# mLSTM output with tokens on the partitions: weighted scores stationary, a one-column denominator per block, and four transposes back

## The reference

```
b      = cumsum(log_sigmoid(f))                 per token i
g_j    = i_j - b_j,   r_i = max(0, max_{j<=i} g_j),   m_i = b_i + r_i
s_ij   = (q_i . k_j) / 8 * exp(g_j - r_i)        for j <= i, else 0
num_i  = sum_j s_ij v_j                          128 values per token
den_i  = sum_j s_ij
h_i    = num_i / max(|den_i|, exp(-m_i))
out_i  = h_i * sigmoid(o_i)
```

## Time and profile before

| | |
|---|---|
| median of 3 executions | 2916.95 us (2909.89 to 2918.77) |
| the profiled execution's own time | 2915.71 us |
| its span from first to last instruction | 2913.9 us |
| PE busy / PEld busy | 2749.6 us (94%) / 2169.3 us (74%) |
| DVE / ACT / POOL busy | 1304.5 us (45%) / 1024.4 us (35%) / 1069.6 us (37%) |
| mean granted TensorE clock | 0.979 of full speed |
| the four heads, layer 1 / layer 2 | 757.79 to 845.34 us / 2200.2 to 2289.2 us of the span |

### The profile page before, as it was taken

One profiled execution on the slowest core, in us unless ns is written; L12 is line 12 of the kernel. 1 busy time (PEld: TensorE's weight loads), 2 busy tenths in 40 slices (PEclk: granted clock), 3 DMA queues, 4 the chain that ended last, 5 costly groups with the idle time before them and its releaser, 6 DMA issues.

```text
span 2913.9 us, 36798 instructions
## 1 busy us (share of the span) xinstructions
PE 2749.6 (94%) x13092; PEld 2169.3 (74%) x13092; DVE 1304.5 (45%) x1596; ACT 1024.4 (35%) x1498; POOL 1069.6 (37%) x450
## 2 busy tenths in 40 slices
PE   6999999999988999999999999999998889999998
PEld 5888877766666787888878888767665667878887
DVE  6333353444655455332353333444454563653322
ACT  3222233555535433222232222244554454332221
POOL 3444444411222343444434444443112223444443
PEclk9999999999989999999999999999998999999999
DMA  3222222211111132223222222232011112222231
GB/s 134 89 99 103 99 87 97 100 45 34 53 45 44 66 108 92 88 100 114 89 73 101 96 100 92 87 108 87 30 44 44 55 44 76 101 92 99 88 119 68
DMA packets 36070, 239.54 MB, mean 82 GB/s; under 512 B 3952, under 2 KB 5232, under 8 KB 13936
## 3 DMA queue, kind: packets, MB, share of 16 engines
q1 hardware_dynamic: 32720, 232.80, 22.7%
q10 hardware_dynamic: 3232, 5.17, 0.5%
HBM read 234.81 MB, written 2.10 MB: 81 GB/s over the span
## 4 chain that ended last, share of the span: by engine, by line
issue 63%; POOL 24%; PE 11%; POOLq 1%; DVE 0%; DVEq 0%
POOL wlo L265 24%; PE bank L1191 4%; PE bank L1192 4%; PE bank L1193 4%; POOLq L264 1%; POOLq L260 1%; DVE hlo L689 0%; DVE x L759 0%; POOL selr L252 0%; DVE hhi L687 0%; POOLq L265 0%; POOLq L256 0%; POOL ones L249 0%; POOL onesm L250 0%; DVEq L759 0%
## 5 line engine op out<-in xcount | busy, mean ns | idle before, releaser
L265 POOL TENSOR_TENSOR wlo<-raw,whi 128x1024 fp32r<-128x1024 f32 (+2 forms) x440 | 1068.0, 2429 | 1825.2 <-ACT whi L298 926.1
L1191 PE MATMUL bank<-hhi,whi 128*128 128x512 f32 x1984 | 798.4, 402 | 48.3 <-POOL wlo L265 36.7
L1193 PE MATMUL bank<-hhi,wlo 128*128 128x512 f32 x1984 | 777.8, 392 | 0.0
L1192 PE MATMUL bank<-hlo,whi 128*128 128x512 f32 x1984 | 777.5, 392 | 0.0
L289 ACT ACTIVATE whi<-raw 128x1024 fp32r<-128x1024 f32 (+1 forms) x232 | 264.0, 1138 | 717.8 <-PE bank L1193 717.6
L1191 PEld LDWEIGHTS bank<-hhi,whi 128*128 128x128 f32 x1984 | 376.4, 190 | 137.9 <-issue 47.2
L1193 PEld LDWEIGHTS bank<-hhi,wlo 128*128 128x128 f32 x1984 | 375.5, 189 | 79.5
L1192 PEld LDWEIGHTS bank<-hlo,whi 128*128 128x128 f32 x1984 | 376.3, 190 | 75.0 <-issue 3.1
L746 DVE TENSOR_TENSOR tmp<-tmp,bank 128x512 f32<-128x512 f32 x80 | 55.0, 688 | 534.0 <-PE bank L1193 534.0
L1191 PE MATMUL bank<-uhi,whi 128*128 128x512 f32 x704 | 274.3, 390 | 0.0
L1193 PE MATMUL bank<-uhi,wlo 128*128 128x512 f32 x704 | 273.9, 389 | 0.0
(11 more groups left out here) (266 smaller groups left out, 3148.9 us busy)
## 6 DMA issues: line engine op xcount, KB each, us to landing
raw<-gu SPq DMA_DIRECT2D x88, 1024.0 KB, 4.8
raw<-dn SPq DMA_DIRECT2D x32, 1408.0 KB, 6.0
raw<-cb SPq DMA_DIRECT2D x48, 768.0 KB, 4.3
raw<-pM SPq DMA_DIRECT2D x16, 1024.0 KB, 4.7
raw<-cq SPq DMA_DIRECT2D x16, 1024.0 KB, 4.8
raw<-pA SPq DMA_DIRECT2D x12, 1024.0 KB, 4.7
raw<-wo SPq DMA_DIRECT2D x8, 1024.0 KB, 4.8
x<-xT ACTq DMA_DIRECT2D x4, 512.0 KB, 9.7
```

The source lines that it names most:

```text
L265: pool.tensor_tensor(wlo[:, s, 0:w], raw[:, j, lo:lo + w], whi[:, s, 0:w].bitcast(f32), ALU.subtract).then_inc(sem["lo_done"], 1)
L1191: mm(outp, wh, mhi, start=start and k == 0, stop=False)
L1192: mm(outp, wh, mlo, start=False, stop=False)
L1193: i = mm(outp, wl, mhi, start=False, stop=stop and k == len(parts) - 1)
```

## The change

1. **Numerator.** The weighted scores become the stationary tile (128x128 blocks of `dm`), the values move: ten matmuls of 128 columns instead of four of 512, 384, 256 and 128. Bank 5 then has the tokens on the partitions.
2. **Denominator.** Blocks of `tmp[:, 4]` are stationary, and two columns of ones move: four small matmuls instead of one of 512 columns. There is one denominator per partition and block.
3. **exp(-m)** is computed once for all heads on 128x16 (tokens on partitions), from four more small transposes, into `st4[:, 0]`; the spreading matmul of m (L1490) and the 128x512 Exp of each head (L548) go. `rows` holds r alone.
4. **DVE** does the two maxima and the reciprocal on 128x4; the product with bank 5 spreads the four reciprocals.
5. **Transposes.** PE transposes the result back into bank 6 (4 of 128x128), and DVE multiplies from there with the gate.
6. **Waits.** PE no longer waits for `h_out` before bank 5; it waits for `h_out` ahead of the transposes, for `h_gated` ahead of the scores in bank 6, and, before the first head, for the one Exp (`em_exp`), which reads bank 4.

```diff
+        row1 = within("row1", VS + 1, [NH, S])
+        em = st4[:, 0].rearrange("p (a h) -> p a h", h=NH)
+        den = st4[:, 1:4, 0:NB]
 ACT
                 act.wait_ge(sem["rt_ready"], me.next("rt_ready"))
+                A(st4[:, 0], bank[4][:, NB * NH:2 * NB * NH], ACT.Exp, scale=-1.0).then_inc(sem["em_exp"], 1)
                 for h in range(NH):
...
-                    act.wait_ge(sem["mm_mm"], me.next("mm_mm"))
-                    if h:
-                        act.wait_ge(sem["h_out"], me.at("h_out", h))
-                    A(tmp[:, 5], bank[6][:], ACT.Exp, scale=-1.0).then_inc(sem["em_exp"], 1)
 DVE
-                dve.tensor_copy(rows[0:NH], tmp[0:NH, 2:4]).then_inc(sem["dve_step"], 1)
+                dve.tensor_copy(rows[0:NH], tmp[0:NH, 2]).then_inc(sem["dve_step"], 1)
...
-                    dve.scalar_tensor_tensor(tmp[:, 5], bank[6][:], -1.0, tmp[:, 5], ALU.mult, ALU.max).then_inc(sem["dve_step"], 1)
+                    sums = bank[6][:, 0:2 * NB].rearrange("p (a b) -> p a b", b=2)[:, :, 0]
+                    dve.scalar_tensor_tensor(den[:, 0], sums, -1.0, em[:, :, h], ALU.mult, ALU.max).then_inc(sem["dve_step"], 1)
-                    dve.tensor_tensor(tmp[:, 5], bank[6][:], tmp[:, 5], ALU.max).then_inc(sem["dve_step"], 1)
+                    dve.tensor_tensor(den[:, 1], sums, den[:, 0], ALU.max).then_inc(sem["dve_step"], 1)
-                    dve.reciprocal(tmp[:, 4], tmp[:, 5]).then_inc(sem["dve_step"], 1)
+                    dve.reciprocal(den[:, 2], den[:, 1]).then_inc(sem["dve_step"], 1)
-                    dve.tensor_tensor(tmp[:, 3], bank[5][:], tmp[:, 4], ALU.mult).then_inc(sem["h_out"], 1)
-                    dve.wait_ge(sem["h_out"], me.next("h_out"))
+                    dve.tensor_tensor(tmp[:, 3].rearrange("p (a b) -> p a b", a=NB), bank[5][:].rearrange("p (a b) -> p a b", a=NB),
+                                      den[:, 2].unsqueeze(2).broadcast_to([P, NB, P]), ALU.mult).then_inc(sem["h_out"], 1)
+                    fill_combine(0, 11 + 4 * h)
                     dve.wait_ge(sem["og_ready"], me.at("og_ready", h + 1))
-                    dve.tensor_tensor(zm[:, 8 + h], tmp[:, 3], zm[:, 8 + h], ALU.mult).then_inc(sem["h_gated"], 1)
+                    dve.wait_ge(sem["h_t"], me.next("h_t"))
+                    dve.tensor_tensor(zm[:, 8 + h], bank[6][:], zm[:, 8 + h], ALU.mult).then_inc(sem["h_gated"], 1)
                     dve.wait_ge(sem["h_gated"], me.next("h_gated"))
-                    fill_combine(0, 11 + 4 * h)
 PE
+                pe.wait_ge(sem["em_exp"], me.at("em_exp", 1))
                 pe.wait_ge(sem["cv_silu"], me.at("cv_silu", 4))
                 for h in range(NH):
...
-                    if h:
-                        pe.wait_ge(sem["h_out"], me.at("h_out", h))
...
-                    mm(bank[6][:], sel(h), rows[:, 1], start=True, stop=True).then_inc(sem["mm_mm"], 1)
                     fill("cb0", 8 + 4 * h)
                     fill("cb0", 9 + 4 * h)
                     pe.wait_ge(sem["d_exp"], me.next("d_exp"))
-                    pe.wait_ge(sem["em_exp"], me.next("em_exp"))
+                    if h:
+                        pe.wait_ge(sem["h_gated"], me.at("h_gated", h))
...
-                    for jt in range(NB):
-                        i = mm(bank[5][:, jt * P:S], zm[:, 4 + h, jt * P:(jt + 1) * P], dm[jt], start=jt == 0, stop=jt == NB - 1)
+                    for it in range(NB):
+                        for jt in range(it + 1):
+                            i = mm(bank[5][:, it * P:(it + 1) * P], dm[jt][:, (it - jt) * P:(it - jt + 1) * P],
+                                   zm[:, 4 + h, jt * P:(jt + 1) * P], start=jt == 0, stop=jt == it)
...
-                    mm(bank[6][:], ones[:], tmp[:, 4], start=True, stop=True).then_inc(sem["den_mm"], 1)
+                    for it in range(NB):
+                        i = mm(bank[6][:, 2 * it:2 * it + 2], tmp[:, 4, it * P:(it + 1) * P], ones[:, 0:2], start=True, stop=True)
+                    i.then_inc(sem["den_mm"], 1)
                     fill("cb0", 11 + 4 * h)
+                    pe.wait_ge(sem["h_out"], me.at("h_out", h + 1))
+                    transposes(bank[6], tmp[:, 3]).then_inc(sem["h_t"], 1)
```

More of the change, by code:

```diff
@@ L150, in build @@
         dm = [tail[0][:, 0:S], tail[1][:, 0:3 * P], tail[1][:, 3 * P:5 * P], tail[0][:, S:S + P]]
-        rows = within("rows", VS, [HD, 2, S], f32r)
+        rows = within("rows", VS, [HD, S], f32r)
+        row1 = within("row1", VS + 1, [NH, S])
+        em = st4[:, 0].rearrange("p (a h) -> p a h", h=NH)
+        den = st4[:, 1:4, 0:NB]
         row0 = within("row0", last, [NH, S])
@@ L195, in build @@
             "cv": 16, "cv_silu": 4, "og_ready": 4, "vm_mm": 8, "vm_ready": 8,
-            "mb_mm": 4, "md_mm": 4, "mm_mm": 4, "d_exp": 4, "em_exp": 4, "sm_mm": 12, "sd_mul": 16, "num_mm": 4, "den_sum": 4, "den_mm": 4,
-            "h_out": 4, "h_gated": 4,
+            "mb_mm": 4, "md_mm": 4, "d_exp": 4, "em_exp": 1, "sm_mm": 12, "sd_mul": 16, "num_mm": 4, "den_sum": 4, "den_mm": 4,
+            "h_out": 4, "h_t": 4, "h_gated": 4,
             "al_mm": 2, "al_abs": 2, "al_e": 2, "al_l": 2, "al_out": 2, "al_b": 2, "sr_ready": 4, "ad_zero": 1,
@@ L988, in _ @@
                 dve.wait_ge(sem["dve_step"], me.next("dve_step"))
-                dve.tensor_tensor(tmp[0:NH, 3], tmp[0:NH, 5], tmp[0:NH, 2], ALU.add).then_inc(sem["dve_step"], 1)
+                dve.tensor_tensor(row1[:], tmp[0:NH, 5], tmp[0:NH, 2], ALU.add).then_inc(sem["dve_step"], 1)
                 dve.memset(rows[:].bitcast(f32), 0.0).then_inc(sem["dve_step"], 1)
@@ L996, in _ @@
                 dve.wait_ge(sem["sel_set"], me.at("sel_set", 1))
-                dve.tensor_copy(rows[0:NH], tmp[0:NH, 2:4]).then_inc(sem["dve_step"], 1)
+                dve.tensor_copy(rows[0:NH], tmp[0:NH, 2]).then_inc(sem["dve_step"], 1)
                 dve.wait_ge(sem["dve_step"], me.next("dve_step"))
-                dve.tensor_tensor(rows[32:32 + NH], tmp[0:NH, 2:4], rows[0:NH].bitcast(f32), ALU.subtract).then_inc(sem["row_m"], 1)
+                dve.tensor_tensor(rows[32:32 + NH], tmp[0:NH, 2], rows[0:NH].bitcast(f32), ALU.subtract).then_inc(sem["row_m"], 1)
                 dve.wait_ge(sem["row_m"], me.next("row_m"))
@@ L1472, in _ @@
                 pe.sem_inc(sem["held"], 1)
-                for a in range(NB):
-                    i = pe.transpose(bank[4][:, a * NH:(a + 1) * NH], row0[0:NH, a * P:(a + 1) * P], ident[0:NH, 0:NH])
+                for e, row in enumerate((row0, row1)):
+                    for a in range(NB):
+                        i = pe.transpose(bank[4][:, (NB * e + a) * NH:(NB * e + a + 1) * NH], row[0:NH, a * P:(a + 1) * P],
+                                         ident[0:NH, 0:NH])
                 i.then_inc(sem["rt_mm"], 1)
@@ L1483, in _ @@
                     q, k = zm[r, h // 2], zm[r, 2 + h // 2]
-                    mm(bank[4][:], sel(h), rows[:, 0], start=True, stop=True).then_inc(sem["mb_mm"], 1)
+                    mm(bank[4][:], sel(h), rows[:], start=True, stop=True).then_inc(sem["mb_mm"], 1)
                     mm(bank[7][:], k[:, 0:P], q, start=True, stop=True).then_inc(sem["sm_mm"], 1)
-                    if h:
-                        pe.wait_ge(sem["h_out"], me.at("h_out", h))
-                    mm(bank[5][:], sel(h), rows[:, 0], start=True, stop=False)
+                    mm(bank[5][:], sel(h), rows[:], start=True, stop=False)
                     mm(bank[5][:], identb, mask_ji.unsqueeze(1).broadcast_to([P, NB, P]), start=False, stop=True).then_inc(sem["md_mm"], 1)
-                    mm(bank[6][:], sel(h), rows[:, 1], start=True, stop=True).then_inc(sem["mm_mm"], 1)
                     fill("cb0", 8 + 4 * h)
@@ L1511, in _ @@
                 fill("cb1", 3)
-                pe.wait_ge(sem["h_out"], me.at("h_out", 4))
+                pe.wait_ge(sem["h_gated"], me.at("h_gated", 4))
                 pe.wait_ge(sem["al_b"], me.at("al_b", 2))
```

2 lines of the change are left out of this document (1 added, 1 removed).

## The result

| | before | changed |
|---|---|---|
| median of 6 runs, us | 2913.35 (2909.89 to 2918.77) | 2892.73 (2890.01 to 2899.45) |
| profiled execution, its own time / span, us | 2915.71 / 2913.9 | 2890.27 / 2888.5 |
| mean granted TensorE clock | 0.979 | 0.987 |

The changed kernel takes 0.9939 of the time before (95% interval 0.9923 to 0.9956): 17.8 us less, between 12.8 and 22.4. The medians lie 20.6 us apart, the two profiled executions 25.4 us. Forecast were 18.0 us less and 2898 us.

What follows compares the result with a forecast made beforehand. PE, busy 94% of the span, was taken to bound the kernel. Terms -10.5 -13.8 -2.7 +0.7 +2.7 +7.6 -2.0 sum to -18.0 us, predicting 2898 us, range 2886 to 2912.

Steps and rivals of the forecast that it cites:

- The wait for `h_out` at bank 5 goes: PE's idle time ahead of heads 2 to 4 disappears: 5.23 us a layer, 10.5 us in all.
- The clock behind it: Heads 2 to 4 return to full PE clock once PE does not stop: 6.92 us a layer, 13.8 in all.
- The rival in which the clock is not given back: Small passes in every head keep PE's clock low, so the 13.8 us are not won: 2911.5 us; chance 0.18.
- The spreading of m goes: Matmul L1490 drops out of each head: 0.34 us each, 8 times, 2.7 us less.
- Numerator: In each head, 20 passes of 128 columns replace 8 passes, 2.2 us against 2.15: +0.05 us, between 0 and +0.3.
- Denominator: In each head, 8 passes bound by weight loads replace two, 0.9 us against 0.86: +0.04 us.
- Transposes: Four new PE transposes cost 0.45 us in heads 1 to 3, 2.7 us in all; head 4's are hidden.
- The new wait before head 1: PE waits for the small Exp: +5.0 us, less 1.2 from DVE; +3.8 us a layer, +7.6 in all.
- The clock in head 1: Clock loss in head 1 becomes 3.06 us a layer, 2.0 us less than before over both layers.
- The wait only moves: DVE is late at the transposes and PE stops there instead; gain shrinks by 12 us to 2910; chance 0.07.
- Slower, because PE starts cold and never gets warm: The wait before head 1 starts PE cold and heads 2 to 4 stay slow: +16.3 us, 2932; chance 0.06.
- The change does not do what it says: PE stops elsewhere in the head, for ACT's Exps or a split tile: 7 us less gain, 2905; chance 0.05.

Runs made afterwards that it cites:

- e1: Kernel before, arithmetic kept, with a fill of 12 matmuls moved ahead of the h_out wait in heads 2 to 4; 2888.95 us, ratio 0.9922.
- e3: Changed kernel with an unused 512-column reciprocal added on DVE ahead of the product in each head; 2922.39 us, ratio 1.0045.
- e7: The changed kernel run again, unaltered, in a later group; 2893.96 us, ratio 0.9932.
- e2: Changed kernel, but DVE's copy takes all 32 columns of bank 4 and the small Exp reads that copy; 2887.10 us, ratio 0.9921.
- e5: e2 with the four Sigmoids moved behind the first head's second split on ACT; 2886.72 us, ratio 0.9908.
- e6: e5 with head 1 started after the third Silu and DVE's bank 4 copy ahead of the last convolution; 2875.98 us, ratio 0.9877.
- e8: e2 run again, unaltered, beside the changed kernel; 2886.53 us, ratio 0.9909.
- e9: e6 with ACT splitting the second fill's tile ahead of the fourth Silu; 2872.26 us, ratio 0.9866.
- e10: e6 run again, unaltered, in the last group; 2877.52 us, ratio 0.9880.
- e4: Changed kernel with an unused 384-column reciprocal added on DVE ahead of the product in each head; 2904.05 us, ratio 0.9977.

## Why the prediction was right

**"The wait for `h_out` at bank 5 goes": right.** 10.5 us of idle time were forecast to go, and heads 2 to 4 have none. DVE's chain was put at 1.4 us and a fill at 2.8; they take 1.3 (779.27 to 780.57) and 2.85, and the transposes never wait, in either layer. What stands behind is hidden too, as said: `h_gated` and the next combine end no idle time.

**"The clock behind it": right, and shown by experiment.** All six heads stand at 1.00, with transposes, 8 denominator passes and 20 numerator passes in each. e1 has the same clock without any of these, and e3 takes it away again by a stop alone. The rival in which the clock is not given back falls.

Of the two terms together, 24.3 us, e1 allows a check: its heads 2 to 4 are 66.32 - 55.33 = 11.0 us a layer shorter than in the kernel before, 11.6 without its own 0.6 us, and 12.15 were forecast. Of the 11.6, 5.2 are the stops themselves and 6.4 what came behind them, where 6.92 were forecast. PEclk has two digits, and three windows of over 21 us can be off by 0.1 us each through that alone.

**"The spreading of m goes": right in sign, too small.** It was priced by one distance, 0.34 us. The part of the second head from its first small matmul to the scores, with 24 dense matmuls in it, takes 6.87 us in the changed kernel (782.48 to 789.35). In e1, with m's spreading and the same 24, it takes 8.13 (779.77 to 787.90), of which about 0.2 is due to e1's order. So the term is worth about 1.1 us in that head, not 0.34. PE's timeline of e1, the second of the two pieces and the dense matmul behind:

```profile
783.77 0.50 PE L1489 MATMUL bank<-rows,selr 64*128 64x512 f32 x1
784.20 0.39 PE L1490 MATMUL bank<-conb 128*128 128x512 bf16 x1
784.52 0.49 PE L1491 MATMUL bank<-rows,selr 64*128 64x512 f32 x1
784.94 0.50 PE L1247 MATMUL bank<-hhi,whi 128*128 128x512 f32 x1
```

The spread of m takes 0.42 us from its start to the next. The rest is likely that the dense matmul can follow the bf16 mask within 0.04 us (783.54 to 783.58 in the changed kernel), which no longer has a small f32r matmul behind it; that was not tried by itself. In the ledger's third line this term and the two below should have come to +0.4 us; they came to -26.7 + 2 x 11.6 = -3.5, and nearly all of the difference is this term.

**"Numerator", "Denominator": right.** Forecast 2.20 and 0.90 us by the weight loads' 0.11 us each, measured 2.23 and 0.82. Before, they took 2.15 and 0.46 to the next start; the prediction's 0.86 has 0.40 us in it by which the dense matmul behind is slow (0.63 to the one after it, where 0.23 is usual). In the changed kernel this one is slow by 0.08 only. To the second dense matmul behind them the two take 3.35 us (793.70 to 797.05) against e1's 3.24 (792.25 to 795.49): +0.1 a head, as forecast.

**"Transposes": right.** 0.45 forecast; from their first to the next start it is 0.53 (781.95 to 782.48), but they also take away the slower step from a dense matmul to the head's first small one: from the last dense matmul to the head's first it is 0.76 us (799.36 to 800.12), in e1 0.32, so 0.44. In head 4 they fall into PE's wait for `cb1`, whole: from its last dense matmul to the first of `cb1` it is 3.87 us in both kernels (835.09 to 838.96, 844.94 to 848.81).

**"The new wait before head 1": right in kind, 0.6 us a layer too small.** From the memset the start is 4.4 us later in both layers of both executions, where 3.8 was forecast. From the last Silu's start on, the wait adds 5.2 us (5.0 forecast): load, four Sigmoids and load as in the earlier trace rows, small Exp 0.18. The last Silu is only 0.8 us earlier (24.2 us from the memset, 25.0 before), not 1.2. No drain beyond a load shows, at neither of the two loads: the Sigmoid starts 0.01 us after the first, the Exp 0.02 after the second. Since both stand in this wait, the 1.4 us that the prediction names for a drain would have come twice. PE stood for 8.35 us, not for the nearly 6 that I named, because the other end of the stop moved as well: it came there at 753.47.

**"The clock in head 1": right.** 0.87 in both layers of the first execution, 0.13 x 20.66 = 2.7 us lost each; e7's heads are at 0.84 and 0.6 us longer, 3.4 lost. The 3.06 that was forecast lies between. A stop of 8.4 us did not make the clock behind it worse than the shorter one had.

**Forecast at nothing: what follows the heads.** The ledger's fifth line is 2.4 us in both executions. It goes with the stop ahead of it, 3.04 us instead of the 3.48 of before, for the last four transposes now stand in that wait, and a clock of 0.90 instead of 0.84. In the traces of the changed kernel, e7, e2, e5, e6, e8, e9 and e10, all with the stop of 3.04 us, 13 of the 16 such stretches took 17.7 to 18.0 us and three 19.2 to 20.3; in the kernel before and e1, with 3.48, the four took 19.1 to 21.0. So it is likely the change's, though no run changed that stop alone. The sixth line is not: the changed kernel's first execution has this, behind a stop that is in the kernel before as well, with 1.61 us for the same eight matmuls there,

```profile
856.90 1.13 PE L1543 MATMUL bank<-tmp 64*128 64x256 f32 x8 [2.44 <-DVE tmp L1118]
857.97 0.50 PE L1249 MATMUL bank<-ohi,whi 128*128 128x512 f32 x1
```

and e7, the same kernel, this:

```profile
855.52 2.08 PE L1543 MATMUL bank<-tmp 64*128 64x256 f32 x8 [2.44 <-DVE tmp L1118]
857.53 0.80 PE L1249 MATMUL bank<-ohi,whi 128*128 128x512 f32 x1
```

The stop is 2.44 us in both, and behind it one works at 2.4 GHz and the other at 1.2.

**The sum.** The two executions of the changed kernel lie 25.4 and 19.5 us below that of before, 22.5 on average, and that of before was 2.4 us above its median: some 20 us, as the medians have it (20.6), and inside the interval of the ratio, whose middle is 17.8. So the 18.0 us of the forecast are a little low, and it came this near because its misses partly cancel: the arithmetic of the heads was put some 4 us too dear and up to 2.4 us behind the heads were not foreseen, but waiting and clock together were put 1 us too high and head 1's start 1.1 us too cheap. (By its own sum the forecast from the median of 2916.95 is 2899, not 2898.)

**The rivals.** "The wait only moves": e4 shows what it would have cost, had DVE been 2.5 us later. "Slower, because PE starts cold and never gets warm": the start is as cold as feared, 8.35 us, and the second head is at 1.00. "The change does not do what it says": no stop for ACT in any head.

## What to carry to other kernels

A dense engine that stops for 1.6 us may pay more for the time behind the stop than for the stop, so look at PEclk in the window behind each wait before pricing it, and look for a place for the wait ahead of which there is work that doesn't depend on it. Here moving 12 matmuls gave what a rewrite of the output gave (e1). When an operation is moved ahead of an engine's start, count all that stands in its queue; and where the wait is only for a buffer to be read, let an engine that passes there anyway take the data out (e2), then follow the next releaser, one by one (e6, e9).

## What the runs showed of the hardware

- The same stop, in the same kernel, lowers the clock in one execution and not in another: L1543 takes 1.13 or 2.08 us behind 2.44 us of idle time. A difference of a few us between two profiled executions needs a second execution of each before it is explained.
- Stops of 1.6 to 1.8 us (before) lowered the granted clock behind them in all six heads, those of 1.9 to 2.2 (e3) in four of six, those of 1.1 to 1.4 (e4) in none of six. But one of 1.35 us, 0.7 us behind another of 0.4 to 0.5, lowered it in one layer of the kernel before and not in the other.
- An f32 matmul that moves 2 columns costs what its stationary tile costs to load: 8 passes in 0.82 us, and eight loads in 0.97 with the last one's 0.19.
- DVE's reciprocal takes 0.18 us for 4 columns and 3.35 for 512, while an elementwise product of 512 columns from PSUM takes 0.69. Per column it is by far the dearest operation of these heads, and tokens on partitions make it vanish.
